# Forgetting attention of the prompt, two heads to a step: 16 double steps in place of 32 single ones

## What is computed

```python
def block(qp, qb, cqb):                       # 8 heads of 64, 512 query rows, causal
    s = jnp.einsum('bqhd,bkhd->bhqk', qb, k_all).astype(jnp.float32)
    s = s + cqb.transpose(0, 2, 1)[..., None] - c_keys      # cumulative log forget values
    s = jnp.where(qp[:, None] >= kpos[None, :], s, NEG_INF)
    p = jax.nn.softmax(s, axis=-1).astype(v_all.dtype)
    return jnp.einsum('bhqk,bkhd->bqhd', p, v_all)
```

## Time and profile before

| what | value |
|---|---|
| median of three runs | 2528.32 us |
| the profiled execution: its time / its span | 2530.0 us / 2528.2 us |
| TensorE (PE) busy | 2433.6 us, 96% of the span |
| VectorE (DVE) busy | 1658.5 us, 66% |
| ScalarE (ACT) busy | 1168.0 us, 46% |
| GpSimd (POOL) busy | 146.7 us, 6% |
| mean granted TensorE clock | 0.989 |
| prompt part of the even attention, first sums to first L1030 | 670.53 to 749.00 us |

### The profile page before, as it was taken

One profiled execution on the slowest core, in us unless ns is written; L12 is line 12 of the kernel. 1 busy time (PEld: TensorE's weight loads), 2 busy tenths in 40 slices (PEclk: granted clock), 3 DMA queues, 4 the chain that ended last, 5 costly groups with the idle time before them and its releaser, 6 DMA issues.

```text
span 2528.2 us, 37287 instructions
## 1 busy us (share of the span) xinstructions
PE 2433.6 (96%) x13811; PEld 2151.9 (85%) x13811; DVE 1658.5 (66%) x2733; ACT 1168.0 (46%) x2111; POOL 146.7 (6%) x217
## 2 busy tenths in 40 slices
PE   7999999999999999999999999999988899999998
PEld 5999987886777899987789998777777677999887
DVE  6777647666666877745687774563235868777545
ACT  4455435344445555534545553452223655555444
POOL 1000001100002000001000000100001420000000
PEclk9999999999999999999999999999997999999999
DMA  4333334421304233334423323443244042333345
GB/s 132 98 84 84 109 124 164 117 73 52 111 19 126 74 89 92 89 124 132 159 70 91 92 85 125 133 146 125 79 125 117 9 142 72 93 87 84 108 133 175
DMA packets 259138, 261.87 MB, mean 104 GB/s; under 512 B 25568, under 2 KB 214000, under 8 KB 258977
## 3 DMA queue, kind: packets, MB, share of 16 engines
q1 hardware_dynamic: 254224, 243.83, 31.9%
q0 software_dynamic: 4464, 14.80, 1.7%
q10 hardware_dynamic: 288, 1.10, 0.1%
HBM read 249.11 MB, written 10.58 MB: 103 GB/s over the span
## 4 chain that ended last, share of the span: by engine, by line
PE 83%; DVE 9%; ACT 3%; issue 2%; DMA 1%; POOL 1%; SPq 0%; ACTq 0%; DVEq 0%
PE ps L972 13%; PE ps L973 13%; PE ps L974 13%; PE ps L1030 5%; PE ps L1031 5%; PE ps L1032 5%; PE ps L1443 3%; PE ps L1445 3%; PE ps L1444 3%; PE ps L1089 2%; PE ps L1091 2%; PE ps L1090 2%; PE ps L965 2%; PE ps L1999 1%; PE ps L1650 1%
## 5 line engine op out<-in xcount | busy, mean ns | idle before, releaser
L972 PE MATMUL ps<-xb,w_all 128*128 128x320 f32 x2176 | 673.7, 310 | 8.8 <-ACT scratch L705 6.4
L973 PE MATMUL ps<-xb,w_all 128*128 128x320 f32 x2176 | 673.1, 309 | 0.0
L974 PE MATMUL ps<-xb,w_all 128*128 128x320 f32 x2176 | 673.0, 309 | 0.0
L533 DVE TENSOR_TENSOR w_all<-raw,w_all 128x1024 fp32r<-128x1024 f32 (+1 forms) x204 | 208.0, 1020 | 362.3 <-ACT w_all L543 196.9
L972 PEld LDWEIGHTS ps<-xb,w_all 128*128 128x128 f32 x2176 | 409.0, 188 | 11.7 <-issue 11.7
L974 PEld LDWEIGHTS ps<-xb,w_all 128*128 128x128 f32 x2176 | 409.1, 188 | 0.0
L973 PEld LDWEIGHTS ps<-xb,w_all 128*128 128x128 f32 x2176 | 409.1, 188 | 0.0
L527 ACT ACTIVATE w_all<-raw 128x1024 fp32r<-128x1024 f32 (+1 forms) x204 | 182.5, 895 | 439.2 <-PE ps L1032 237.4
L636 DVE TENSOR_TENSOR w_all<-raw,w_all 128x512 fp32r<-128x512 f32 x364 | 251.5, 691 | 145.4 <-ACT w_all L629 144.5
L629 ACT ACTIVATE w_all<-raw 128x512 fp32r<-128x512 f32 x364 | 229.2, 630 | 182.0 <-PE ps L974 139.2
L1030 PE MATMUL ps<-w_all 128*128 128x512 f32 x528 | 205.9, 390 | 0.9 <-DVE w_all L548 0.9
(11 more groups left out here) (379 smaller groups left out, 4192.8 us busy)
## 6 DMA issues: line engine op xcount, KB each, us to landing
raw<-in_w_ffn_out SPq DMA_DIRECT2D x176, 512.0 KB, 3.3
raw<-in_w_ffn_in SPq DMA_DIRECT2D x120, 512.0 KB, 4.7
gain<-in_w_ffn_in SPq DMA_DIRECT2D x56, 512.0 KB, 4.2
raw<-in_w_in_odd SPq DMA_DIRECT2D x56, 256.0 KB, 2.7
raw<-in_w_out_even SPq DMA_DIRECT2D x16, 512.0 KB, 3.4
raw<-in_w_out_odd SPq DMA_DIRECT2D x16, 512.0 KB, 3.5
gain<-in_norm_g POOLq DMA_DIRECT2D x12, 512.0 KB, 6.6
raw<-in_w_in_even SPq DMA_DIRECT2D x24, 256.0 KB, 2.6
```

The lines of the kernel that those rows point to most:

```text
L533: return nc.vector.tensor_tensor(lo, raw[:, RAW[u][0], 0:n], hi.bitcast(F32), ALU.subtract)
L972: nc.tensor.matmul(dst, wl, xh[:, k, :], start=fresh and k == 0, stop=False, skip_group_check=True)
L973: nc.tensor.matmul(dst, wh, xl[:, k, :], start=False, stop=False, skip_group_check=True)
L974: mm = nc.tensor.matmul(dst, wh, xh[:, k, :], start=False, stop=(k == HK - 1), skip_group_check=True)
```

## The change

The even attention gets functions of its own (`pe_prompt_even`, `act_prompt_even`, `dve_prompt_even`), and the odd one keeps the old code with its branches for even taken out. A double step is block i of the heads 2c and 2c + 1, 16 in all:

- QK of both heads stand one after the other, the one on rows 0 to 63, the other on rows 64 to 127, into two banks: (0, 1) or, in every other step, (5, 7).
- VectorE still adds the forget terms head by head, but the mask, the maximum, the reciprocal and the division cover both heads in one instruction each.
- ScalarE's exponentials stay one per head; the copy after T covers both heads.
- T of both heads fills banks 2 and 3 and is no longer double-buffered; PV of both heads shares bank 4, no longer double-buffered either.
- Sums of the next pair come after the QK of blocks 2 and 3. T runs two double steps behind QK, PV three.
- The scores move out of `att` into a stretch of SBUF that is free at that time (`x_free`), and `negc` now has room for four heads.

```diff
+        x_free = at_byte("x_free", 0, [P, 4096], back=8 * BLOCK)
-        negc = view(scratch, 0, 2, 512)
-        stE = view(att, 0, 4, 512)
-        ptE = view(att, 2048, 2, 4, P)
+        negc = [view(att, 2048, 2, 512), view(scratch, 0, 2, 512)]
+        stE = view(x_free, 0, 4, 2, 512)
+        ptE = view(att, 0, 2, 2, 4, P)
...
+        def sc_banks(n):
+            return (0, 1) if n % 2 == 0 else (5, 7)
+        def pe_prompt_even(pe):
+            d = BEHIND
...
+            for j in range(len(PAIRS) + d + 1):
+                if j < len(PAIRS):
+                    n, i, c = PAIRS[j]
+                    w = (i + 1) * P
+                    if n == 0:
+                        pe.wait_ge(pn_done, 1)
+                        sums(0)
+                    if n == 1:
+                        pe.wait_ge(hl_copied, 1)
+                    if n >= 2:
+                        pe.wait_ge(s_read, 2 * (n - 1))
+                    for m in range(2):
+                        mm = nc.tensor.matmul(bank(sc_banks(n)[m], w), qTE[64 * m:64 * m + 64, c, i * P:(i + 1) * P],
+                                              kTE[64 * m:64 * m + 64, c, 0:w], start=True, stop=True)
+                    mm.then_inc(qk_mm, 2)
+                    if i >= NP - 2 and c + 1 < CL:
+                        sums(2 * (c + 1) + i - (NP - 2))
+                    if n == 0:
+                        sums(1)
+                        pe_sample_own(pe, 0)
+                    if n == 1:
+                        pe_sample_turn(pe, 0)
+                if d <= j < len(PAIRS) + d:
+                    n, i, c = PAIRS[j - d]
+                    pe.wait_ge(p_done, 2 * (n + 1))
+                    if n:
+                        pe.wait_ge(pt_done, 2 * n)
...
+                if j > d:
+                    n, i, c = PAIRS[j - d - 1]
+                    pe.wait_ge(pt_done, 2 * (n + 1))
+                    if n:
+                        pe.wait_ge(o_done, 2 * n)
...
+        def act_prompt_even(act):
...
+            for j in range(len(PAIRS) + d):
+                if j == 0:
+                    sums(0)
+                    sums(1)
+                if d <= j:
...
+                    nc.scalar.activation(ptE[:, n % 2, :, 0:i + 1, :], ps[:, 2:4, 0:w].rearrange("p m (k n) -> p m k n", n=P),
+                                         ACT.Copy).then_inc(pt_done, 2)
+                if j < len(PAIRS):
...
+                    for m in range(2):
+                        e = nc.scalar.activation(stE[:, n % 4, m, 0:w], stE[:, n % 4, m, 0:w], ACT.Exp,
+                                                 bias=rneg[:, m, r], accum_out=rsum[:, m, r])
+                    e.then_inc(p_done, 2)
+                    if i >= NP - 2 and c + 1 < CL:
+                        sums(2 * (c + 1) + i - (NP - 2))
...
+        def dve_prompt_even(dve):
...
+                if i == 0:
+                    dve.wait_ge(nc_done, 2 * (c + 1))
...
+                for m in range(2):
+                    h = 2 * c + m
+                    nc.vector.scalar_tensor_tensor(s_t[:, m, 0:w], bank(sc_banks(n)[m], w), cq[:, i, h:h + 1],
+                                                   negc[c % 2][:, m, 0:w], ALU.add, ALU.add).then_inc(s_read, 1)
...
+                last = s_t[:, :, i * P:w]
+                link(dve, nc.vector.tensor_tensor(last, last, con[:, C_NT:C_NT + P].unsqueeze(1).to_broadcast([P, 2, P]),
+                                                  ALU.add))
+                nc.vector.tensor_reduce(rneg[:, :, r], s_t[:, :, 0:w], AX.X, ALU.max, negate=True).then_inc(s_ready, 2)
...
+                nc.vector.tensor_tensor(heads, bank(4, P).rearrange("p (m e) -> p m e", e=DH),
+                                        rinv[:, :, n % 4:n % 4 + 1].to_broadcast([P, 2, DH]), ALU.mult).then_inc(o_done, 2)
...
+                if j == 0:
+                    dve_sample_own(dve, 0)
+                if j == 1:
+                    dve_sample_rows(dve, 0)
```

More of the change, by code:

```diff
@@ L1937, in pe_prompt, with pe_prompt_odd @@
+        def pe_prompt_odd(pe):
+            g0 = NSTEP
+            d = BEHIND
             for j in range(NSTEP + d + 1):
                 if j < NSTEP:
-                    n, i, h = st[j]
+                    n, i, h = STEPS[j]
                     g = g0 + n
                     w = (i + 1) * P
[L1942 to L1966, removed]
@@ L1967, in pe_prompt @@
                     mm.then_inc(qk_mm, 1)
-                    if not odd and i == NP - 2 and h + 1 < NH:
-                        sums(h + 1)
                     if n == 1:
-                        pe_sample_own(pe, odd)
+                        pe_sample_own(pe, 1)
                     if n == 2:
-                        pe_sample_turn(pe, odd)
+                        pe_sample_turn(pe, 1)
                 if d <= j < NSTEP + d:
-                    n, i, h = st[j - d]
+                    n, i, h = STEPS[j - d]
@@ L1991, in pe_prompt, with act_prompt_odd @@
                     elif n == 0:
[L1993 to L1997, removed]
+                        pe.wait_ge(sot_done, 2)
+                    b = 6 + n % 2
+                    pt = ptO[:, n % 2]
                     for kb in range(i + 1):
-                        mm = nc.tensor.matmul(bank(b, w), pt[:, kb, :], v[:, kb, h * w:(h + 1) * w],
+                        mm = nc.tensor.matmul(bank(b, P), pt[:, kb, :], vO[:, kb, h * P:(h + 1) * P],
                                               start=(kb == 0), stop=(kb == i))
                     mm.then_inc(pv_mm, 1)
[L2003 to L2019, removed]
+        def act_prompt_odd(act):
+            g0 = NSTEP
+            d = BEHIND
+            for j in range(NSTEP + d + 2):
                 if d <= j < NSTEP + d:
-                    n, i, h = st[j - d]
+                    n, i, h = STEPS[j - d]
                     g = g0 + n
@@ L2081, in combine @@
                 dve.wait_ge(p_done, g + 1)
-                if not odd:
-                    if n >= 4:
-                        dve.wait_ge(o_done, g - 3)
-                    nc.vector.reciprocal(rinv[:, 0, r], rsum[:, 0, r]).then_inc(c_done, 1)
-                    return
                 p1, p2 = pO[:, n % 3, 0, 0:w], pO[:, n % 3, 1, 0:w]
@@ L2589, in _ @@
             pe_sample(pe, 1)
-            pe_prompt(pe, 1)
+            pe_prompt_odd(pe)
             for j in range(3):
```

193 lines of the change are left out of this document (117 added, 76 removed).

## The result

Over 20 runs of each, the changed kernel takes 2534.14 us (2529.9 to 2537.46) and the kernel before 2529.41 (2528.26 to 2531.44). The ratio is 1.0018, with a 95% interval of 1.0012 to 1.0024. I had forecast 2522.5, a gain of 5.8 us; the kernel lost 4.7 and lies outside the range that I gave. It also scatters 7.6 us from run to run where the kernel before scatters 3.2.

What follows compares the result with a forecast made beforehand. TensorE's queue was taken to bound the kernel: -11.8 (QK overlap) - 1.8 (fewer groups) + 7.8 (added waits) = -5.8 us, so 2524.2 against the profiled execution and 2522.5 as median; range 2519.5 to 2529.5.

Steps and rivals of the forecast that it cites:

- QK side by side: TensorE, even attention: two heads' QKs overlap fully, so a pair's four cost 2.94 us, not 5.88; saves 11.8 us.
- Fewer groups: TensorE's T and PV go from 32 groups to 16 with the same blocks; saves 1.8 us, between 1.1 and 2.2.
- My work terms: TensorE's work in the even attention before: eight heads 72.3 us, plus low-clock first sums and sample pieces, 76.5.
- Waits: TensorE's waits at five places of the even attention: 9.8 us against about 2.0 before, so 7.8 more.
- the second sums: Start of the even attention: the second group of sums waits 0.5 us for ScalarE's copy of the first.
- the sums of head 3: They wait once, 2.15 us, for the copy of head 2's sums, which stands behind an exponential on ScalarE.
- T of block 3 and PV of block 2: T waits for block 2's copy, PV for VectorE's division: 0.6 to 0.9 us in each of three pairs, 2.1 together.
- the tail: After the last QK, T 14, PV 13, T 15 and PV 15 each wait for a copy or division: 3.8 us together.
- The part, 72.7: The even attention, from first sums to output projection, should take 72.7 us against 78.5 before.
- The clock falls at the new waits: Rival: TensorE's granted clock falls once or twice at the added waits, 1.6 to 3.5 us dearer, 2525; chance 0.20.
- The last rival: Clock stays low after one fall at about 687 us; all 52 us left would give 2545; chance 0.05.
- The gain should be kept: Behind the even attention: TensorE's queue follows with its first two weight tiles ready as before, so the 5.8 us remain.

Runs made afterwards that it cites:

- parted: The changed kernel with one small matmul on all 128 rows between the QKs of a step's two heads; 2541.90 us.
- both: The changed kernel with ScalarE's copies of the sums ahead of the exponentials and unread matmuls in TensorE's waits of the last steps; 2522.13 us.
- copies_first: The changed kernel with ScalarE's copies of the sums put ahead of the same step's exponentials; 2528.67 us.
- before_single: The kernel before, with T waiting for the copy and PV for the division of the step just before; 2545.70 us.
- by_head: The changed kernel with VectorE's mask, maximum, reciprocal and division again one instruction per head; 2530.38 us.
- banked: copies_first with more banks for T 14, PV 13 and PV 15, and unread matmuls only ahead of T 15 and PV 15; 2522.82 us.

## Why the prediction was wrong

- **QK side by side, -11.8.** Right: 1.06 for 512 keys of two heads; "parted" takes it away. The four widths of a pair take 3.1 us in place of 2.94 (0.50, 0.71, 0.85 and 1.06, the second less a wait of 0.27), so the saving was some 0.7 us smaller, an estimate.
- **Fewer groups, -1.8.** Not measured by itself. In "both", at full clock, the part is 69.8 us. My work terms (76.5 - 11.8 - 1.8 = 62.9), the 2.8 us of bracketed waits that are left and 4.0 us of filler, from start to start, make 69.7.
- **Waits, +9.8 against 2.0.** Right in place, releaser and size: 0.27 for the second sums (0.5 forecast), 1.24 for L1718 (1.2), 2.00 for the sums of head 3 (2.15), 2.2 for T of block 3 and PV of block 2 (2.1), 3.3 for the tail (3.8). VectorE's wide forms took what I had set: the mask 425 ns, the maximum over 1024 columns 1222, over 768 columns 955.
- **The part, 72.7.** At full clock it is right, by this estimate. By the sums (4.2 at the low clock for 2.3) a low us costs 0.44 us (the first profile's rows at the end give 0.42 for T of eight blocks, 742.26 to 743.80 against 0.90, and 0.46 for the last PV), so the 14.4 low us of the first profile are 6.3 and the 13.2 of the second 5.8: 80.0 - 6.3 = 73.7 and 78.4 - 5.8 = 72.6. The same rate takes copies_first's 73.4 to 69.7, the part of "both" (69.8).
- **The step that failed** is the sum itself, which counts every wait at its length and puts the clock at nothing: that was left to the rival "The clock falls at the new waits". I gave it 0.20, argued that "the waits are broken up by work", and priced it at 1.6 to 3.5 us for one or both falls, from the shortest low stretch I had (3.3 us) and the first sums. Both falls came in both profiles of the changed kernel, in stretches of 3.4 to 14 us, the second of which runs 2.3 to 3.5 us into the matmuls of the projection: 17.1 low us in each profile, 7.5 us by the rate. That is more than the 5.8 us of expected gain. I had the warning in the earlier trace rows: 1.98 busy of 4 us had been enough around 2012. The tail that I had laid out with 3.8 us of waiting in 7.6 was the same share, and I should have counted it as a fall, not as a chance.
- **The last rival**, which I gave 0.05, had the right arithmetic (13 low us use the gain up, 25 make the kernel 0.2% slower) on another mechanism: the clock did not stay low after one fall, it fell twice and came back each time. Its "52 us that are left" from 687 should have been 56.
- **"The gain should be kept"** failed too. Between 640 and 775 us the two profiles of the changed kernel lost 2.7 and 1.7 us, of 6.9 and 4.1 us in all; the rest lies in stages that didn't change, behind 775 us (4.2 and 0.9) and in the second profile ahead of 640 (1.5, with a low stretch of 3.4 us at 494 that before hasn't). In the whole execution the first profile has some 27 us more at the low clock than before; at 0.44 that is 12, which leaves 5 us of gain against the 5.8 forecast.
- **The same at an equal clock.** "Both" has about the clock of before. The forecast's -5.8, less 2.8 us of waits removed and with 0.7 us by which the filler (4.0) exceeds the tail's waits (3.3), gives -7.9; measured -7.8. By these estimates work and waits were forecast rightly, and the clock alone turned the result.

## What to carry to other kernels

Where TensorE sets the pace, an edit that shortens its work but opens its queue must be summed in two currencies: the length of each wait, and the half clock that can follow it; here the second, 7.5 us by an estimate, was larger than the whole expected gain of 5.8. Keep two buffers between TensorE and the engines that empty its banks (going to one cost the kernel before 16 us), put copies that TensorE waits for ahead of longer work on the copying engine, and in a tail that can't be covered let TensorE run unread matmuls. Here the last two took a 0.2% loss to a 0.3% gain with the edit's idea unchanged.

## What I had not expected of the hardware

Added work made the kernel faster: about 4 us of matmuls whose result nobody reads took 5.8 us off its median. Very short waits can cost the clock: in before_single, brackets of 0.35 us, one per head, went with 26 of its 29.5 us at 1.2 GHz (the first 3.4 followed a wait of 1.18), although the busy share of the stretch read 3.65 of 4. Matmul records overlap, so such a share hides idling: T of two blocks, 0.27 from start to start in the earlier trace rows, took 0.79 there (724.31 to 725.10), with only 0.35 of it in the bracket.

What stays open: by_head has as much bracketed waiting as the changed kernel and still one fall less, and neither the 1.41 us in banked nor the 1.18 us at the end of the kernel before brought a fall. So I can say which stretches fell but not give a rule for when one will. Nor is it settled why the clock is low for longer in the unchanged stages of the other kernels, which lose 1.3 us on average behind the change; a kernel that only shifts the later stages in time, at several offsets, would tell, and was not run.
